# A one-core layer pair whose expert stream is spread over VectorE's steps: four stream pieces a step in tile 2's second attention, and an even tile's projection, norm and queries one step earlier

## The chip, the cores and the metric

The kernel runs on one core of one Trainium2 chip. The metric is the device time of one execution in microseconds (us). Engines: PE is TensorE, DVE is VectorE, ACT is ScalarE, POOL is GpSimd, SP is SyncE.

## What is computed

Two layers in a row over 512 tokens of width 1024, in float32.

```python
x = first_block(x, ...)     # 16 meta tokens, windowed pooling, forgetting attention, gates, norm
h = rms_norm(x, attn_norm); proj = h @ w_in
sb = stick_breaking_attention(sb_q, sb_k, sb_v)         # 8 heads
mla = chunk_causal_softmax_attention(q, k, v)           # 8 heads
x = x + concat(rms_norm(sb), rms_norm(mla)) @ w_o
x = x + peer_ffn(rms_norm(x, ffn_norm), ...)

def peer_ffn(...):                                       # per token
    q = (x @ w_q).reshape(T, 8, 2, 128)
    sc = einsum('thcd,chnd->thcn', q, sub_keys)          # 8 heads, 2 halves, 128 keys
    top_s, top_i = top_k(sc, 16)                         # then the best 16 of 256 pairs
    g = softmax(best_s)
    pre = einsum('td,thkd->thk', x, u[idx])              # 128 rows of u per token
    out = einsum('thk,thkd->td', g * gelu(pre), v[idx])  # 128 rows of v per token
```

u and v have 16384 rows of 1024 numbers each. What bears on the change is the second attention (stick-breaking and softmax), the projection by w_o, the queries of the expert layer, its top-k and its dot products with rows of u.

## The kernel before, in words

**Tiles and groups.** The 512 tokens are four tiles of 128, numbered 0 to 3. Group 0 is tiles 0 and 1, group 1 is tiles 2 and 3. "The third tile" is tile 2. For each group the program runs first_dense, first_attention, first_output, second_dense and second_attention; PE, ACT and DVE each have their own function of that name, with the same loops, and meet at semaphores. After both groups the expert stage proper follows: PE builds weights ("builds") and multiplies streamed tiles of v by them.

**The second attention** has one step for each tile and head, p = 0 to 15 in a group. In a step DVE takes the positive part (L1670), runs the reversed scan (L1672), subtracts (L1678), takes the next head's maximum (L1657, L1658), lets the stream go on by two pieces (`side(2)`), normalises the softmax (L1685, L1686), on an even head copies out the outputs of the two heads before (`outputs`, L1626), and lets the stream go on again. PE forms the scores of head p+2, which wait for DVE's L1678 of head p, then transposes head p's probabilities (L2054), which wait for L1686; it multiplies by the values one step later. ACT has the exponentials and copies the transposed probabilities.

**What rides along in the odd tile's steps.** While tile 1 (or 3) is in its attention, the even tile before it gets its output projection (`project` on PE, four of 8 matmuls of 512 columns, each followed by `combine` on DVE, L1644; all four use one PSUM bank, so a project waits for the combine before it), its norm (`expert_norm` on ACT, `prep_norm` on DVE, L1651), and ten pieces of preparation (`prepare` on PE, `evac_prep` on ACT, L894): two transposes xT, four queries q of 32 matmuls each, four scores s. Three tables say at which head h each stands: PROJECT_AT, PREP_AT and the `h ==` lines. Below, P1, P2 and P3 are the three steps in which PE does three preparations each. The odd tile has the same work after its last head.

**The stream.** `experts()` is a Python generator that emits DVE's expert work piece by piece, and `side(n)` emits the next n pieces at that place in DVE's order. A piece is a dot (L1206, one gathered row of u for each of 128 tokens against the token) or one of the eleven parts of a pair: the top-k of two heads (`prep_pair`, L1122 to L1195). I count these parts 0 to 10. A pair can't begin before its scores are copied out by ACT, and `routed` says from which step it may stand in the order; until then a `side` emits nothing. POOL gathers the rows of u (L656) when a pair has given the indices (L1195). The first 256 dots use six buffers, so a gather waits for the dot six before it.

**The hand-over.** After dot 256 (head-chunk 15) the stream takes a pair (heads 16 and 17), and then, in the program before, nothing until both groups' attention is over. What follows emits 14 dots of chunk 16, the pair of heads 18 and 19, the last two dots of chunk 16, and the first build. The last two rows of chunk 16 go into buffers that are free only when PE's last preparation is done.

Of the kernel before, what the change touches and what calls it, by code (L numbers as in the profile page):

```python
# [24 lines left out]
H = 8  # L25
# [39 lines left out]
def build(nc, a, out):  # L65

    ctx = ExitStack()
    with ctx:
# [146 lines left out]
        KEYS = range(len(gathered), len(gathered) + 2 * (first_at - keys_at) // D)  # L215
# [149 lines left out]
        PREP = [("xT", 0), ("xT", 1), ("q", 0), ("q", 1), ("s", 0), ("q", 2), ("s", 1), ("q", 3), ("s", 2), ("s", 3)]  # L365
        NP = len(PREP)

        PROJECT_AT = {2: (0, 1), 3: (2, 3)}
        PREP_AT = {5: (0, 1, 2), 6: (3, 4, 5), 7: (6, 7, 8)}


        w_in = a["w_in"][0]
# [290 lines left out]
        def _(act):  # L663
# [246 lines left out]
            def second_attention(g):  # L910
# [30 lines left out]
                for p in range(first, end):  # L941
                    i, h = ATT[p]
                    w = (i + 1) * P
                    if p + 1 < end:
                        softplus(p + 1)
                    if p > first:
                        copy_pT2(p - 1, 0)
                        copy_pT2(p - 1, 1)
                    if i % TG:
                        if h == 2:  # L950
                            out_root(i - 1)
                        if h == 4:
                            expert_norm(i - 1)
                        for n in PREP_AT.get(h, ()):
                            evac_prep(i - 1, n)
                    act.wait_ge(ml_max, p + 1)
                    if p:
                        act.wait_ge(pT2_done[1], p)
                    nc.scalar.activation(Pb2[:, 1, 0:w], psum[:, 2 + p % 2, 0:w], ACT.Exp,
                                         bias=stat[:, 96 + p % 4:97 + p % 4], scale=QK ** -0.5,  # L960
                                         accum_out=stat[:, 100 + p % 4:101 + p % 4]).then_inc(exp2_done[1], 1)
                    act.wait_ge(zr_done, p + 1)
                    nc.scalar.activation(Pb2[:, 0, 0:w], Pb2[:, 0, 0:w], ACT.Exp).then_inc(exp2_done[0], 1)
                    if p % 2 == 0 and p > first:
                        squares(p // 2 - 1)
# [3 lines left out]
                i = TG * g + TG - 1  # L969
# [116 lines left out]
        def _(dve):  # L1086
# [23 lines left out]
            routed = [0] * NT  # L1110
# [144 lines left out]
            def experts():  # L1255
                def tops_of(*ks):
                    for k in ks[::2]:
                        while k % H + 1 >= routed[k // H]:
                            yield
                        yield from prep_pair(k // 2)  # L1260
# [7 lines left out]
                    yield from dots(k)  # L1268
                split()
                early_over[0] = True  # L1270
                yield from tops_of(2 * H, 2 * H + 1)
                while not dense_over[0]:
                    yield
                first_rows = dots(16)
                for _ in range(len(KEYS) + 4):
                    next(first_rows)
                yield from tops_of(18, 19)
                for _ in first_rows:
                    pass
                beside = chain(*[dots(k) for k in U_FIRST])  # L1280
                for b in range(BUILDS):
# [73 lines left out]
            def side(n):  # L1355
                for _ in range(n):
                    next(stream, None)
# [260 lines left out]
            def second_attention(g):  # L1618
# [43 lines left out]
                for p in range(first, end):  # L1662
                    i, h = ATT[p]
# [26 lines left out]
                    if i % TG:  # L1690
                        for n in PROJECT_AT.get(h, ()):
                            combine(i - 1, n)
                        if h == 4:
                            prep_norm(i - 1)
                        routed[i - 1] = {5: 2, 6: 6, 7: 8}.get(h, 0)
                        side(6 if h > 4 else 3)
                    else:
                        side(4)
                outputs(end // 2 - 1)
                i = TG * g + TG - 1  # L1700
                mean_squares(i)
# [563 lines left out]
```

## Time and profile before

| What | Value |
|---|---|
| three runs | 2197.37, 2205.95, 2209.19 us; median 2205.95 |
| profiled execution | 2211.92 us, of which the span of its instructions is 2209.9 us |
| PE busy | 1940.1 us (88%) |
| DVE busy | 1383.5 us (63%) |
| POOL busy | 934.9 us (42%) |
| ACT busy | 547.1 us (25%) |
| the chain that ended last | PE 58%, DVE 12%, POOL 11%, issue 7%, DMA 7%, ACT 3% |

Times within the profile are counted from the span's start. The second attention of group 0 stands at about 371 to 508 us (tile 1 from 397), that of group 1 at about 1028 to 1237 us (tile 3 from 1110), and the first build begins at 1309 us. Busy shares are means over stages that differ, so the change has to be read stage by stage. A row of a timeline gives a start, a length, the engine, the line and the operation, and in brackets how long the engine had been idle and who released it.

### The profile page before, as it was taken

What the parts mean: (1) busy time and instruction counts of PE and PEld (TensorE: products, weight loads), DVE (VectorE), ACT (ScalarE), POOL (GpSimd) and SP (SyncE); (2) the same over time, 40 slices, a digit from 0 to 9 for tenths busy, and PEclk for the clock granted to TensorE, in tenths of its full rate; (3) what the DMA queues carried; (4) which work ended last, traced back from release to release, by engine and by line L of the source; (5) the groups of instructions that cost most, each with busy time, mean ns of one, the idle gap of its engine ahead of it and who ended that gap; (6) DMA issues with size and microseconds to landing.
All of it is one profiled execution on the core that took longest, in us unless ns stands there. A gap on an engine that the chain in (4) does not pass through costs nothing.

```text
span 2209.9 us, 22139 instructions
## 1 busy us (share of the span) xinstructions
PE 1940.1 (88%) x7602; PEld 1231.5 (56%) x7602; DVE 1383.5 (63%) x3090; ACT 547.1 (25%) x1520; POOL 934.9 (42%) x814
## 2 busy tenths in 40 slices
PE   6999999887998998967778878899999999997776
PEld 5677666575865665544657666644457644442222
DVE  1111224455878874768986388899779966634554
ACT  2112024322111110212333237600138610011111
POOL 2000000010335562575761246533868864447775
PEclk9999998798998888986588889999999999999999
DMA  5322344155977797798875677899999999989998
GB/s 173 130 97 82 128 158 152 58 189 198 333 271 256 253 342 260 278 383 292 299 269 215 247 276 239 260 340 354 396 409 317 321 409 409 409 347 409 401 410 358
DMA packets 190623, 614.85 MB, mean 278 GB/s; under 512 B 18096, under 2 KB 18096, under 8 KB 190512
## 3 DMA queue, kind: packets, MB, share of 16 engines
q0 software_dynamic: 111168, 403.64, 49.6%
q1 hardware_dynamic: 76400, 202.92, 24.8%
q10 hardware_dynamic: 2944, 6.89, 0.9%
q8 instruction: 61, 1.00, 0.2%
q14 instruction: 50, 0.41, 0.1%
HBM read 610.22 MB, written 3.15 MB: 278 GB/s over the span
## 4 chain that ended last, share of the span: by engine, by line
PE 58%; DVE 12%; POOL 11%; issue 7%; DMA 7%; ACT 3%; ACTq 0%; POOLq 0%; SPq 0%; DVEq 0%
PE ps L1736 57%; POOL sb_arena L656 9%; DVE sb_arena L1206 4%; DMA sb_arena<-in_peer_u,sb_idx 3%; POOL sb_wring L656 2%; ACT sb_arena L1033 1%; DMA sb_wring<-in_w_out 1%; DMA sb_gains<-in_norm_g 1%; DVE sb_arena L1672 1%; PE ps L2054 1%; DMA sb_wring<-in_w_up_attn 1%; DMA sb_wring<-in_w_in 1%; DVE sb_arena L1346 0%; DMA sb_arena<-in_peer_v,sb_idx 0%; DVE sb_arena L1678 0%
## 5 line engine op out<-in xcount | busy, mean ns | idle before, releaser
L656 POOL DMA_INDIRECT sb_arena<-in_peer_u,sb_idx x470 | 602.8, 1283 | 1035.3 <-DVE sb_idx L1195 482.9
L1736 PE MATMUL ps<-sb_wring,sb_arena 128*128 128x512 f32 (+2 forms) x1632 | 699.5, 589 | 41.8 <-DVE sb_arena L1574 18.2
L1206 DVE CUSTOM_DVE_ANT_0 sb_arena<-sb_arena 128x1024 f32<-128x1024 f32 x470 | 562.4, 1222 | 102.0 <-DMA sb_arena<-in_peer_u,sb_idx 98.2
L1736 PEld LDWEIGHTS ps<-sb_wring,sb_arena 128*128 128x128 f32 x1632 | 312.6, 193 | 418.2 <-issue 365.5
L1736 PE MATMUL ps<-sb_arena,sb_wring 128*128 128x256 f32 (+2 forms) x2688 | 512.9, 353 | 14.6 <-ACT sb_arena L894 5.9
L1736 PEld LDWEIGHTS ps<-sb_arena,sb_wring 128*128 128x128 f32 x2688 | 447.8, 199 | 68.7 <-issue 6.5
L1736 PE MATMUL ps<-sb_arena 128*128 128x64 f32 (+9 forms) x1968 | 350.6, 330 | 57.9 <-DVE sb_arena L1678 16.8
L1736 PEld LDWEIGHTS ps<-sb_arena 128*128 128x128 f32 (+4 forms) x1968 | 279.6, 199 | 123.5 <-issue 73.8
L656 POOL DMA_INDIRECT sb_arena<-in_peer_v,sb_idx x192 | 202.8, 1056 | 121.3 <-PE ps L1736 50.3
L1736 PE MATMUL ps<-sb_arena,sb_poolw 128*128 128x512 f32 (+1 forms) x424 | 204.1, 608 | 56.6 <-DMA sb_arena<-in_peer_v,sb_idx 36.2
L1235 DVE SCALAR_TENSOR_TENSOR sb_arena<-sb_arena,sb_coef 128x1024 f32<-128x1024 f32 x90 | 115.5, 1284 | 118.3 <-DMA sb_arena<-in_peer_v,sb_idx 118.0
L1736 PEld LDWEIGHTS ps<-sb_arena,sb_poolw 128*128 128x128 f32 x424 | 74.0, 192 | 161.6 <-ACT sb_poolw L1024 85.0
L1033 ACT ACTIVATE sb_arena<-sb_arena 128x64 f32<-128x64 f32 x512 | 129.2, 335 | 47.8 <-DVE sb_arena L1346 43.2
L1024 ACT ACTIVATE sb_poolw<-sb_ident,sb_coef 128x128 f32<-128x128 f32 x136 | 53.9, 399 | 282.8 <-PE ps L1736 282.8
L1736 PE MATMUL ps<-sb_wring,sb_poolw 128*128 128x512 f32 x136 | 66.3, 610 | 19.2 <-DMA sb_wring<-in_peer_v,sb_idx 14.0
L656 POOL DMA_INDIRECT sb_wring<-in_peer_u,sb_idx x42 | 50.9, 1211 | 75.0 <-PE ps L1736 43.0
L1349 DVE TENSOR_TENSOR sb_arena<-sb_arena,sb_iota 128x1024 f32<-128x1024 f32 x64 | 77.8, 1216 | 0.0
L656 POOL DMA_INDIRECT sb_wring<-in_peer_v,sb_idx x64 | 66.0, 1031 | 26.9 <-issue 14.3
L1001 ACT ACTIVATE sb_coef<-sb_coef 128x16 f32<-128x16 f32 (+1 forms) x18 | 4.0, 225 | 270.7 <-DVE sb_coef L1206 270.6
L1470 DVE TENSOR_REDUCE sb_stat<-ps 128x1 f32<-128x144 f32 (+3 forms) x32 | 16.2, 507 | 79.7 <-PE ps L1736 78.7
L1206 DVE CUSTOM_DVE_ANT_0 sb_wring<-sb_wring,sb_arena 128x1024 f32<-128x1024 f32 x42 | 51.2, 1224 | 15.8 <-DMA sb_wring<-in_peer_u,sb_idx 15.5
L1235 DVE SCALAR_TENSOR_TENSOR sb_arena<-sb_wring,sb_coef,sb_arena 128x1024 f32<-128x1024 f32 x30 | 38.5, 1284 | 34.9 <-DMA sb_wring<-in_peer_v,sb_idx 34.8
(240 smaller groups left out, 1341.3 us busy)
## 6 DMA issues: line engine op xcount, KB each, us to landing
sb_wring<-in_peer_v SPq DMA_DIRECT2D x128, 512.0 KB, 6.8
sb_wring<-in_w_in SPq DMA_DIRECT2D x52, 1024.0 KB, 7.5
sb_wring<-in_peer_w_q SPq DMA_DIRECT2D x32, 1024.0 KB, 7.4
sb_wring<-in_w_o SPq DMA_DIRECT2D x16, 1024.0 KB, 7.1
sb_wring<-in_w_out SPq DMA_DIRECT2D x8, 1024.0 KB, 9.3
sb_arena<-in_peer_u,sb_idx POOLq DMA_INDIRECT x470, 6.6
sb_arena<-in_x ACTq DMA_DIRECT2D x8, 512.0 KB, 7.0
sb_wring<-in_w_up_pool SPq DMA_DIRECT2D x4, 1024.0 KB, 7.2
```

The lines of the kernel that those rows point to most:

```text
L656: nc.gpsimd.indirect_dma_start(gathered[buf(n)], None, table, bass.IndirectOffsetOnAxis(ap=idx[:, t, at_:at_ + 1], axis=0))\
L1001: nc.scalar.activation(coef[:, t, cols], coef[:, t, cols], ACT.Gelu).then_inc(gelu_done, k1 - k0)
L1024: nc.scalar.activation(diag[:, n % 4, :], ident[:], ACT.Copy, scale=coef[:, t, s:s + 1])\
L1033: last = nc.scalar.activation(pick_a[:, b % 2, n, :], pick_a[:, b % 2, n, :], ACT.Copy, scale=rank_t[:, 2 * TG + t, at_ + n:at_ + n + 1])
L1206: nc.vector.tensor_tensor_reduce(out=gathered[buf(n)], in0=gathered[buf(n)], in1=xn[:, t % TG, :], scale=1.0, scalar=0.0, op0=ALU.mult, op ...
L1235: nc.vector.scalar_tensor_tensor(rows_of_tile(t), gathered[buf(n)], coef[:, t, s:s + 1], rows_of_tile(t), ALU.mult, ALU.add).then_inc(vect ...
L1349: nc.vector.tensor_tensor(pick_j[b % 2], second_.to_broadcast([P, PICK, NK]), iota[:].unsqueeze(1).to_broadcast([P, PICK, NK]), ALU.is_equal)\
L1470: nc.vector.tensor_reduce(stat[:, 96 + n % 4:97 + n % 4], s_ps[:, 0:w], AX, ALU.max, negate=True)\
L1672: link(nc.vector.tensor_tensor_scan(suffix[:, w - 1::-1] if w == T else suffix[:, 0:w][:, ::-1], suffix[:, w - 1::-1] if w == T else suffi ...
L1736: return nc.tensor.matmul(o, l, r, start=start, stop=stop)
L2054: last = nc.tensor.transpose(psum[:, 4 + kind, j * P:(j + 1) * P], Pb2[:, kind, j * P:(j + 1) * P], ident[:])
```

## The change

Three things are edited. In the even tile's steps the second `side` gives two pieces in place of four, so a step has four pieces, not six. Tile 0 shares the line, but no score has been formed then and the stream is empty. In the odd tile's steps all four projections stand at head 2 (before: two at head 2, two at head 3), the norm at head 3 (before 4), the preparations at heads 4, 5 and 6 (before 5, 6 and 7), and `side` gives six pieces from head 4 on (before from 5). The pair of heads 18 and 19 stands right behind that of 16 and 17, where the stream may take it during the attention, and the detour before the first build is gone.

```diff
-        PROJECT_AT = {2: (0, 1), 3: (2, 3)}
-        PREP_AT = {5: (0, 1, 2), 6: (3, 4, 5), 7: (6, 7, 8)}
+        PROJECT_AT = {2: (0, 1, 2, 3)}
+        PREP_AT = {4: (0, 1, 2), 5: (3, 4, 5), 6: (6, 7, 8)}
...
-                        if h == 4:
+                        if h == 3:
                             expert_norm(i - 1)
...
-                yield from tops_of(2 * H, 2 * H + 1)
+                yield from tops_of(*range(2 * H, 2 * H + 4))
                 while not dense_over[0]:
                     yield
-                first_rows = dots(16)
-                for _ in range(len(KEYS) + 4):
-                    next(first_rows)
-                yield from tops_of(18, 19)
-                for _ in first_rows:
+                for _ in dots(16):
                     pass
...
-                        if h == 4:
+                        if h == 3:
                             prep_norm(i - 1)
-                        routed[i - 1] = {5: 2, 6: 6, 7: 8}.get(h, 0)
-                        side(6 if h > 4 else 3)
+                        routed[i - 1] = {4: 2, 5: 6, 6: 8, 7: 8}.get(h, 0)
+                        side(6 if h > 3 else 3)
                     else:
-                        side(4)
+                        side(2)
```

Behind the edit the lines of the rest are four lower (L1736 is L1732, L1686 is L1682, L1626 is L1622, L1644 is L1640).

**On PE, group 0, tile 1, from head 2 on.** The rows of 8 matmuls with `sb_wring` and 512 columns are two projections. Before:

```order
L1736 MATMUL ps<-sb_arena 64x128 x4
L1736 MATMUL ps<-sb_wring,sb_arena 128x512 x8
L1736 MATMUL ps<-sb_arena 128x256
L1736 MATMUL ps<-sb_masks,sb_identb 128x128
L1736 MATMUL ps<-sb_arena 128x256
L1736 MATMUL ps<-sb_masks,sb_identb 128x128
L2054 MATMUL ps<-sb_ident,sb_arena 128x128 x4
L1736 MATMUL ps<-sb_ones,sb_arena 128x1 x2
L1736 MATMUL ps<-sb_arena 64x128 x4
L1736 MATMUL ps<-sb_wring,sb_arena 128x512 x8
```

With the change:

```order
L1732 MATMUL ps<-sb_arena 64x128 x4
L1732 MATMUL ps<-sb_wring,sb_arena 128x512 x16
L1732 MATMUL ps<-sb_arena 128x256
L1732 MATMUL ps<-sb_masks,sb_identb 128x128
L1732 MATMUL ps<-sb_arena 128x256
L1732 MATMUL ps<-sb_masks,sb_identb 128x128
L2050 MATMUL ps<-sb_ident,sb_arena 128x128 x4
L1732 MATMUL ps<-sb_ones,sb_arena 128x1 x2
L1732 MATMUL ps<-sb_arena 64x128 x4
```

The four projections now stand together, and head 3's step has none.

**On DVE, group 1, the end of tile 3's attention.** L1685 and L1686 (L1681 and L1682) normalise head 7, L1626 (L1622) is the last `outputs`, L1632 (L1628) the sum of squares that follows. Before:

```order
L1670 TENSOR_SCALAR sb_arena<-ps 128x512
L1672 SCALAR_TENSOR_TENSOR sb_arena<-sb_arena 128x512
L1678 TENSOR_TENSOR sb_arena<-ps,sb_arena 128x512
L1685 RECIPROCAL sb_stat<-sb_stat 128x1
L1686 TENSOR_SCALAR sb_arena<-sb_arena,sb_stat 128x512
L1626 TENSOR_SCALAR sb_arena<-ps,sb_gains 128x128 x2
L1632 TENSOR_REDUCE sb_stat<-ps 128x2
```

With the change, the rows just ahead of the last `outputs`:

```order
L1193 SCALAR_TENSOR_TENSOR sb_arena<-sb_arena 128x2x16
L1195 CAST sb_idx<-sb_arena 128x32
L1122 MAX sb_arena<-sb_arena 128x8 x4
L1126 MAX_INDEX sb_arena<-sb_arena 128x8 x4
L1130 MATCH_REPLACE sb_arena<-sb_arena 128x128 x2
L1138 MAX sb_arena<-sb_arena 128x8 x2
L1142 MAX_INDEX sb_arena<-sb_arena 128x8 x2
L1130 MATCH_REPLACE sb_arena<-sb_arena 128x128 x2
L1138 MAX sb_arena<-sb_arena 128x8 x2
L1622 TENSOR_SCALAR sb_arena<-ps,sb_gains 128x128 x2
L1628 TENSOR_REDUCE sb_stat<-ps 128x2
```

Between head 7's normalise and the last outputs stand six stream pieces now; they are parts 9 and 10 of one pair and 0 to 3 of the next, and two more pieces stand ahead of the normalise.

**On DVE, between the last two combines of tile 3** (L1640), with the change; before, the four combines follow each other:

```order
L1640 SCALAR_TENSOR_TENSOR sb_arena<-ps,sb_stat,sb_arena 128x512
L1176 CAST sb_angle<-sb_arena 128x64
L1177 CAST sb_angle<-sb_arena 128x64
L1179 TENSOR_SCALAR sb_arena<-sb_angle 128x2x16
L1180 SCALAR_TENSOR_TENSOR sb_arena<-sb_angle 128x2x16
L1181 SCALAR_TENSOR_TENSOR sb_arena<-sb_arena,sb_angle 128x2x16
L1184 TENSOR_TENSOR sb_arena<-sb_arena,sb_iota 128x512
L1189 TENSOR_TENSOR sb_arena<-sb_arena,sb_angle 128x512
L1192 TENSOR_REDUCE sb_arena<-sb_arena 128x32
L1184 TENSOR_TENSOR sb_arena<-sb_arena,sb_iota 128x512
L1189 TENSOR_TENSOR sb_arena<-sb_arena,sb_angle 128x512
L1640 SCALAR_TENSOR_TENSOR sb_arena<-ps,sb_stat,sb_arena 128x512
```

These are parts 8 and 9 of the pair of heads 18 and 19. Between the other combines stand parts 4 to 7.

## Rows read from the trace of the kernel before

**Rows 1.** Windows, seven steps of tile 2 (length, PE, PEld, DVE, ACT, POOL, PEclk, DMA, GB/s):
```profile
1037.84:1110.54 72.70, 56.07 (x208) 44.27 (x208) 71.72 (x139) 26.03 (x59) 54.50 (x43) 0.52 0.89 303
```

**Rows 2.** Timeline of DVE, two dots there (start, length, engine, line, operation):
```profile
1070.95 1.22 DVE L1206 CUSTOM_DVE_ANT_0 sb_arena<-sb_arena 128x1024 f32<-128x1024 f32 x1
1072.09 1.22 DVE L1206 CUSTOM_DVE_ANT_0 sb_arena<-sb_arena 128x1024 f32<-128x1024 f32 x1
```

**Rows 3.** Timeline of PE in one step of it: scores and values:
```profile
1070.44 1.64 PE L1736 MATMUL ps<-sb_arena 64*128 64x256 f32 x4 [1.88 <-DVE sb_arena L1678]
...
1076.11 2.79 PE L1736 MATMUL ps<-sb_arena 128*64 128x128 f32 x12
```

**Rows 4.** Timeline of DVE, tile 3, heads 2 to 4: second combine, two scans:
```profile
1141.94 0.75 DVE L1644 SCALAR_TENSOR_TENSOR sb_arena<-ps,sb_stat,sb_arena 128x512 f32<-128x512 f32 x1 [3.79 <-PE ps L1736]
...
1146.76 1.22 DVE L1672 TENSOR_TENSOR_SCAN sb_arena<-sb_arena 128x512 f32<-128x512 f32 x1
...
1161.66 1.22 DVE L1672 TENSOR_TENSOR_SCAN sb_arena<-sb_arena 128x512 f32<-128x512 f32 x1
```

**Rows 5.** Timelines of DVE and PE, tile 3, heads 5 to 7: waits:
```profile
1199.29 0.87 DVE L1122 MAX8 sb_arena<-sb_arena 128x8 f32<-128x128 f32 x4 [10.66 <-ACT sb_arena L894]
...
1210.64 1.97 PE L2054 MATMUL ps<-sb_ident,sb_arena 128*128 128x128 f32 x8 [3.92 <-DVE sb_arena L1686]
...
1230.18 1.43 PE L2054 MATMUL ps<-sb_ident,sb_arena 128*128 128x128 f32 x8 [2.08 <-DVE sb_arena L1686]
```

**Rows 6.** Timeline of DVE, end of tile 3's attention and last combine:
```profile
1229.64 0.49 DVE L1686 TENSOR_SCALAR sb_arena<-sb_arena,sb_stat 128x512 f32<-128x512 f32 x1
...
1236.42 0.61 DVE L1626 TENSOR_SCALAR sb_arena<-ps,sb_gains 128x128 f32<-128x128 f32 x2 [6.29 <-ACT sb_arena L937]
...
1252.60 0.75 DVE L1644 SCALAR_TENSOR_TENSOR sb_arena<-ps,sb_stat,sb_arena 128x512 f32<-128x512 f32 x1 [2.68 <-PE ps L1736]
```

**Rows 7.** Timeline of DVE, the one whole top-k pair before the first build:
```profile
1285.96 0.87 DVE L1122 MAX8 sb_arena<-sb_arena 128x8 f32<-128x128 f32 x4
...
1290.38 0.49 DVE L1138 MAX8 sb_arena<-sb_arena 128x8 f32<-128x128 f32 x2
...
1292.10 0.50 DVE L1154 MAX8 sb_arena<-sb_arena 128x8 f32<-128x136 f32 x2
...
1295.52 0.20 DVE L1176 CAST sb_angle<-sb_arena 128x64 f32<-128x64 uint16 x1
...
1301.27 0.28 DVE L1195 CAST sb_idx<-sb_arena 128x32 uint32<-128x32 f32 x1
```

**Rows 8.** Timelines of DVE and PE, tile 1: scans, last normalise, outputs, sums:
```profile
425.89 0.69 DVE L1672 TENSOR_TENSOR_SCAN sb_arena<-sb_arena 128x256 f32<-128x256 f32 x1
...
437.64 0.69 DVE L1672 TENSOR_TENSOR_SCAN sb_arena<-sb_arena 128x256 f32<-128x256 f32 x1
...
497.76 0.35 DVE L1686 TENSOR_SCALAR sb_arena<-sb_arena,sb_stat 128x256 f32<-128x256 f32 x1
...
507.03 0.60 DVE L1626 TENSOR_SCALAR sb_arena<-ps,sb_gains 128x128 f32<-128x128 f32 x2
...
507.78 0.98 PE L1736 MATMUL ps<-sb_ones,sb_arena 128*128 128x1 f32 x4 [6.31 <-DVE sb_arena L1626]
```

**Rows 9.** Timelines of DVE and POOL at the start of group 1:
```profile
569.82 1.50 DVE L1376 TENSOR_TENSOR sb_arena<-ps,sb_gains 128x512 f32<-128x512 f32 x2 [1.78 <-PE ps L1757]
...
493.67 0.94 POOL L656 DMA_INDIRECT sb_arena<-in_peer_u,sb_idx  x1 [0.30 <-issue]
...
574.70 1.99 POOL L656 DMA_INDIRECT sb_arena<-in_peer_u,sb_idx  x1 [0.30 <-issue]
```

**Rows 10.** The chain that ended last, before the first build (start, length, what):
```profile
1253.88 40.99 issue
...
1296.34 8.37 DMA sb_wring<-in_peer_u,sb_idx
...
1308.78 12.47 PE ps L1736 x52
```

## The prediction

> **What bounds the kernel now.** I read the page's busy shares first (PE 88%), then the chain that ended last, then windows and timelines of the stretches that the change touches. Each attention step is read by the wait that ends last in it.
>
> In tile 2's second attention DVE is the bound. Seven steps take 72.70, a step 10.39, and DVE is busy for 71.72 of them, PE for 56.07 at a granted clock of 0.52, so nearly always at 1.2 GHz [rows 1]. PE waits for L1678 at each scores [rows 3].
>
> In tile 3, heads 2 and 3 are a round trip: DVE waits 3.79 for a projection and combines it in 0.75 [rows 4], and the next projection needs that bank. From head 5 on PE's preparations are the bound: DVE once waited 10.66 for scores to be copied out, with nothing of the stream to do [rows 5]. At the end of both tiles the stream is dry: after the last normalise DVE has only outputs, and waits 6.29 for ACT [rows 6].
>
> The first build, at 1308.78, is reached through POOL's gathers: 40.99 of issue, a landing of 8.37, one dot [rows 10]. From there on (901 us to the end of the span) the change touches nothing, so I carry the difference at the first build to the end.
>
> **The terms.** Times are of the profiled execution (2211.92, which is 5.97 above the median of 2205.95); I add the sum to either. About 0.5%, 11 us, is what a measurement can tell from no change.
>
> 1. *Tile 2, two dots a step fewer.* Two dots start 1.14 apart [rows 2], so DVE's step falls by 2.29 to 8.10. PE's loop is then next: from its scores to the end of its values, where the next scores stand, is 1070.44 to 1078.90, 8.46 [rows 3], without its present wait of 1.88 before the scores. The step becomes 8.46: −1.93 × 8 = **−15.4**. Bounds: −18.3 if DVE still sets it, −13 if the two engines' waits for each other leave 0.3 a step.
>
> 2. *Tile 3, all projections at head 2.* Two more round trips, 2 × (3.79 + 0.75) = 9.1 [rows 4], move to head 2; the step from head 3's scan to head 4's took 14.90 [rows 4]. If the moved trips cover it, two steps shrink together by 14.90 − 9.1 = **−5.8**. In tile 1 the same is 11.75 [rows 8] − 9.1 = **−2.6**.
>
> 3. *Tile 3, preparations from head 4.* The stall of 10.66 goes [rows 5], but PE had preparations to do in most of it: what PE itself lost is its 3.92 before head 6's transposes against 2.08 in the next step [rows 5]. I take **−1.8** (0 to −3.9).
>
> 4. *The last step of tile 3.* The stream is no longer dry there. Between head 6's normalise and the last outputs DVE's order now has, by count, the parts of a whole pair and parts 1 to 3 of another. A pair is 1285.96 to 1301.55, 15.6; its parts 1 to 3 are 1285.96 to 1290.87 less the first 0.87, 4.0 [rows 7]. With 0.2 off for what does not wait, 19.4, plus DVE's own work of about 4.6 (outputs 0.6, the scan group 2.7, normalise 0.65, outputs 0.6), is 24. Before, from that normalise's end at 1230.13 to the outputs' end at 1237.03 was 6.9 [rows 6]. So the last outputs come **+17** later. Queued behind the pieces are the last normalise, for which PE's transposes wait, and the last outputs, for which PE's sum of squares waits, with tile 3's projection behind it. Nothing is late enough elsewhere to cover it.
>
> 5. *Between the last combines.* The last gap becomes parts 8 and 9, 1295.52 to about 1300.2, 4.7 [rows 7], against an idle 2.68 before [rows 6]: **+2.0**. The gaps before hold cheaper parts, which fit the round trip.
>
> 6. *The last step of tile 1.* The same with a whole pair (15.4) and parts 5 to 7 (3.4 [rows 7]), and own work of 3.2: 22. Before: 498.11 to 507.63, 9.5 [rows 8]. **+12.5**. PE already waited 6.31 for these outputs [rows 8], so nothing covers it either.
>
> 7. *The seam between the groups.* The stream goes into group 1 eight pieces ahead. What stood there was 22 parts and 2 dots; now it is 14 parts and 10 dots in a row, with six buffers. The seventh dot's gather is issued when the first dot is over: POOL needs 1.99 and 0.30 a gather beside dots, 0.94 when DVE is in none [rows 9], and a landing takes 8.37 [rows 10]. Six dots of 1.14 last 6.9, so the seventh waits 3 to 6; DVE has 1.78 of slack before it [rows 9]. **+3** (0 to +6).
>
> 8. *The pair of heads 18 and 19 before the first build.* DVE is rid of 15.6 of work at 1285.96 [rows 7], but the chain there goes over POOL's issue and the landing, not over DVE's pairs [rows 10]: **0**. If the chain could start earlier, at most DVE's part of it, some −4. The gathers into the last two buffers still wait for PE's last preparation, which follows tile 3's projection.
>
> Group 1: −15.4 − 5.8 − 1.8 + 17 + 2 = −4.0. Group 0 and seam: −2.6 + 12.5 + 3 = +12.9. Sum **+9**, so 2205.95 + 9 = **2215** by the median, 2221 by the profiled execution. The change pays in tile 2 and pays back in the two last steps, where it puts VectorE's stream in front of work that PE waits for.
>
> SBUF: by the Trainium skill (SBUF — State Buffer, "Who interferes with whom") a VectorE instruction with two SBUF inputs contends with a GpSimd instruction that reads SBUF, and the later one stands until the first is done. The gathers' 1.99 against 0.94 agree with it [rows 9]; by that rule ten dots in a row are the dearest place for gathers, and with the undisturbed 0.94 the seam would cost about 1 in place of 3.
>
> **The rivals.**
>
> *A, the last steps are covered.* ACT's copies of the last preparations and PE's own step could be what the last outputs wait for, as in tile 3 before (6.29 for ACT [rows 6]); then DVE's pieces fill idle time. Terms 4 to 6 would fall away: 9 − 31.5 = −22.5, 2183. Against it: DVE's count of 24 and 22 is of work alone, and the idle it can fill is 6.29 and already counted. If only half is covered it gives about 2199. Chance 0.15.
>
> *B, slower: gathers can't keep up with dots in a row.* Place: the ten dots at the seam. If every one of the last eight waits for POOL's cadence of 2.29 instead of 1.14 [rows 2, 9], that is 9.2 and not 3, sum +15, 2221; with term 1 at −13 it is +18, 2224. It decides against me from a seam cost of 5 on, as the sum is then past 11. For: POOL is busy 54.50 of 72.70 even at six pieces [rows 1]. Against: the first six rows are there before. Chance 0.20.
>
> *C, PE's clock rises in tile 2.* PE was granted 0.52 with 56.07 of 72.70 busy [rows 1]. With steps of 8.46, PE would hardly idle, and if it is granted 2.4 GHz its loop falls well under 8.10 and DVE stays the bound: −18.3, sum +6, 2212. Against: PE's work was interrupted at every scores [rows 3] and would be still. Chance 0.10. The Trainium skill (TensorE: Matmul & The Clock Gate, "A second HAM failure mode: psum-queue depth-cycling") says that frequent short idle times between groups of matmuls can keep the clock swinging between its two levels; the 0.52 of the row agrees, and by that rule tile 2 stays at the low level as long as PE waits in every step.
>
> *That the change does not do what it says* is excluded for the projections, the pieces and the pairs by the rows of the order; only tile 0, whose stream is empty, doesn't feel the smaller number.
>
> **How the numbers follow.** The forecast case has 0.55. With terms 1, 3, 4 and 7 at their ends it reaches from 2207 to 2224, and it lies at 0.34 within 0.5%, at 0.20 slower and at 0.01 faster. Rival A gives 0.15 faster, B 0.20 slower, C 0.08 within and 0.02 slower. That makes faster 0.16, same 0.42, slower 0.42. The range is 2198 to 2229: below, half of rival A; above, B with another 5 for the medians' scatter (the three runs lie 11.8 apart).
>
> **What would show it.** In the changed kernel's profile: scans of tile 2 about 8.5 apart (10.39 before); no wait of 10.66 for scores in tile 3; the last outputs of group 0 ending near 517 (507.63), with PE waiting some 12 to 17 for them; those of group 1 near 1246; waits of DVE for gathers among the dots right behind group 0; the first build near 1318 (1308.78) and 901 us from there to the end. I am wrong if the outputs at the end of tile 1 come no later than 510 (rival A), if the seam costs over 5 (B), if tile 2 has a granted clock well above 0.52 (C), or if the first build moves by something other than the outputs before it, which would mean that term 8 is not 0.

## The result and the profile after

The changed kernel took 2225.09 us (median of 9 runs, 2208.93 to 2228.67), the kernel before 2206.93 (9 runs, 2197.37 to 2213.66). The ratio is 1.0078, with a 95% interval of 1.0055 to 1.0101: 17 us slower. On a second chip it was 1.0069 (1.0044 to 1.0093). I had forecast 9 us slower; the way it went was right, and its size is twice the forecast's.

The two profiled executions (2211.92 and 2225.09) are read by landmarks. A step is counted from one head's scan to the next.

| Landmark | before | after | late by | of it new |
|---|---|---|---|---|
| last combine of tile 1 | 525.3 | 542.0 | 16.7 | +16.7 |
| first scan of tile 2's second attention | 1027.2 | 1051.0 | 23.8 | +7.1 |
| first scan of tile 3's | 1110.5 | 1115.8 | 5.3 | −18.5 |
| last combine of tile 3 | 1252.6 | 1268.7 | 16.1 | +10.8 |
| first build | 1308.8 | 1325.7 | 16.9 | +0.9 |
| PE's last instruction | 2205.0 | 2218.3 | 13.3 | −3.6 |

**Tile 2.** The windows of its seven steps (columns as in [rows 1]):

```profile
1059.35:1115.83 56.48, 46.29 (x211) 37.61 (x210) 55.51 (x111) 25.90 (x60) 35.39 (x28) 0.69 0.77 253
```

A step takes 8.07 in place of 10.39 [rows 1]. DVE is busy for 55.51 of 56.48, so it still is the bound, and PE was granted 0.69 and not 0.52.

**The steps of heads 2 and 3.** Timeline of DVE, the scans of heads 2, 3 and 4 in tile 1; head 2's of before; and the same four in tile 3 (the others of before are in [rows 4] and [rows 8]):

```profile
407.27 0.69 DVE L1668 TENSOR_TENSOR_SCAN sb_arena<-sb_arena 128x256 f32<-128x256 f32 x1
...
434.80 0.69 DVE L1668 TENSOR_TENSOR_SCAN sb_arena<-sb_arena 128x256 f32<-128x256 f32 x1
...
441.45 0.69 DVE L1668 TENSOR_TENSOR_SCAN sb_arena<-sb_arena 128x256 f32<-128x256 f32 x1
```

```profile
407.60 0.69 DVE L1672 TENSOR_TENSOR_SCAN sb_arena<-sb_arena 128x256 f32<-128x256 f32 x1
```

```profile
1135.80 1.22 DVE L1668 TENSOR_TENSOR_SCAN sb_arena<-sb_arena 128x512 f32<-128x512 f32 x1
...
1163.44 1.22 DVE L1668 TENSOR_TENSOR_SCAN sb_arena<-sb_arena 128x512 f32<-128x512 f32 x1
...
1174.91 1.22 DVE L1668 TENSOR_TENSOR_SCAN sb_arena<-sb_arena 128x512 f32<-128x512 f32 x1
```

```profile
1130.51 1.22 DVE L1672 TENSOR_TENSOR_SCAN sb_arena<-sb_arena 128x512 f32<-128x512 f32 x1
```

Head 2's step grew from 18.3 to 27.5 in tile 1 and from 16.2 to 27.6 in tile 3. Head 3's step shrank, but only from 11.8 to 6.6 and from 14.9 to 11.5. So the two together are longer with the projections packed. With them each odd tile can be split by its scans:

| Stretch | tile 1 before | tile 1 after | tile 3 before | tile 3 after |
|---|---|---|---|---|
| first scan to head 2's | 9.7 | 9.7 | 20.0 | 20.0 |
| head 2's to head 4's | 30.0 | 34.2 | 31.2 | 39.1 |
| head 4's to the last combine | 87.7 | 100.6 | 90.9 | 93.8 |

**The end of tile 1.** Timeline of DVE, from head 6's normalise to the last outputs, and of PE, which waits twice there:

```profile
502.03 0.35 DVE L1682 TENSOR_SCALAR sb_arena<-sb_arena,sb_stat 128x256 f32<-128x256 f32 x1
...
515.55 0.35 DVE L1682 TENSOR_SCALAR sb_arena<-sb_arena,sb_stat 128x256 f32<-128x256 f32 x1
...
523.42 0.61 DVE L1622 TENSOR_SCALAR sb_arena<-ps,sb_gains 128x128 f32<-128x128 f32 x2
```

```profile
515.96 1.12 PE L2050 MATMUL ps<-sb_ident,sb_arena 128*128 128x128 f32 x4 [10.43 <-DVE sb_arena L1682]
...
524.17 0.97 PE L1732 MATMUL ps<-sb_ones,sb_arena 128*128 128x1 f32 x4 [2.96 <-DVE sb_arena L1622]
```

From 502.38 to 524.03 are 21.7. The 9.5 of [rows 8] is not the same place: it starts at head 7's normalise. Head 6's of before is this row:

```profile
480.38 0.35 DVE L1686 TENSOR_SCALAR sb_arena<-sb_arena,sb_stat 128x256 f32<-128x256 f32 x1
```

From its end, 480.73, to 507.63 are 26.9, with PE's last three preparations in them. So this stretch became 5.2 shorter, not longer; from head 7's normalise on it is 8.1 in place of 9.5. What the pieces do cost shows in PE: it has no preparation left for this step and stands for 10.43 and 2.96, where it stood 1.80 and 6.31 before.

**The first preparation step of tile 1.** Timeline of PE, transposes and first query:

```profile
445.05 1.12 PE L2114 MATMUL ps<-sb_ident,sb_arena 128*128 128x128 f32 x4 [0.68 <-ACT sb_arena L894]
446.89 10.06 PE L1732 MATMUL ps<-sb_arena,sb_wring 128*128 128x128 f32 x64 [0.72 <-ACT sb_arena L894]
```

The 64 matmuls took 10.06; in the profile of the kernel before, taken again in experiment 11, they took 7.38 and the transposes 0.65 instead of 1.12. Over the 32 us from the first transpose the granted clock was 0.86 here and 1.00 there.

**The seam.** Timeline of DVE, two of the ten dots behind group 0:

```profile
579.10 1.22 DVE L1206 CUSTOM_DVE_ANT_0 sb_arena<-sb_arena 128x1024 f32<-128x1024 f32 x1
...
582.97 1.23 DVE L1206 CUSTOM_DVE_ANT_0 sb_arena<-sb_arena 128x1024 f32<-128x1024 f32 x1 [2.64 <-DMA sb_arena<-in_peer_u,sb_idx]
```

Six dots run without a wait, and the seventh waits 2.64.

**The end of tile 3.** Timeline of DVE, the last two normalises, the last outputs and the last combine; then PE:

```profile
1228.20 0.49 DVE L1682 TENSOR_SCALAR sb_arena<-sb_arena,sb_stat 128x512 f32<-128x512 f32 x1
...
1242.99 0.49 DVE L1682 TENSOR_SCALAR sb_arena<-sb_arena,sb_stat 128x512 f32<-128x512 f32 x1
...
1251.61 0.61 DVE L1622 TENSOR_SCALAR sb_arena<-ps,sb_gains 128x128 f32<-128x128 f32 x2
...
1268.67 0.75 DVE L1640 SCALAR_TENSOR_TENSOR sb_arena<-ps,sb_stat,sb_arena 128x512 f32<-128x512 f32 x1
```

```profile
1243.53 1.97 PE L2050 MATMUL ps<-sb_ident,sb_arena 128*128 128x128 f32 x8 [9.43 <-DVE sb_arena L1682]
```

From 1228.69 to 1252.22 are 23.5. Here too the 6.9 of [rows 6] starts at head 7's normalise, and head 6's of before is this row:

```profile
1210.09 0.49 DVE L1686 TENSOR_SCALAR sb_arena<-sb_arena,sb_stat 128x512 f32<-128x512 f32 x1
```

From its end to 1237.03 are 26.5, so this stretch is 3.0 shorter, and from head 7's normalise on it is 8.7 in place of 6.9. PE stands for 9.43 in front of head 7's transposes, 2.08 before [rows 5]. The last combine starts 5.2 after the one at 1263.46 and waits for nothing but the pieces in front of it; before it followed after 3.4 with an idle 2.68 [rows 6].

### The profile page after: what moved, and what is told of

Read it like the earlier page. It is cut to its first block, busy times and chain, and to the rows that moved or that the text cites. A ratio compares the mean times of both kernels' runs of the same rounds, so it can differ in the third digit from the quotient of the medians.

```text
span 2223.3 us, 22142 instructions
## 1 busy us (share of the span) xinstructions
PE 1938.9 (87%) x7602; PEld 1231.5 (55%) x7602; DVE 1382.9 (62%) x3090; ACT 547.3 (25%) x1520; POOL 935.7 (42%) x814
## 3 DMA queue, kind: packets, MB, share of 16 engines
q0 software_dynamic: 111168, 403.64, 49.0%
## 4 chain that ended last, share of the span: by engine, by line
PE 59%; DVE 12%; POOL 10%; DMA 8%; issue 7%; ACT 4%; ACTq 0%; POOLq 0%; DVEq 0%; SPq 0%
PE ps L1732 57%; POOL sb_arena L656 8%; DMA sb_arena<-in_peer_u,sb_idx 3%; DVE sb_arena L1206 3%; POOL sb_wring L656 2%; ACT sb_arena L1033 1%; DMA sb_arena<-in_peer_v,sb_idx 1%; DMA sb_wring<-in_w_out 1%; DMA sb_gains<-in_norm_g 1%; PE ps L2050 1%; DMA sb_wring<-in_w_up_attn 1%; DVE sb_arena L1668 1%; DMA sb_wring<-in_w_in 1%; DVE sb_arena L1342 0%; DVE sb_arena L1184 0%
## 5 line engine op out<-in xcount | busy, mean ns | idle before, releaser
L1732 PE MATMUL ps<-sb_wring,sb_arena 128*128 128x512 f32 (+2 forms) x1632 | 697.1, 588 | 44.6 <-DVE sb_arena L1570 18.7
L1732 PEld LDWEIGHTS ps<-sb_wring,sb_arena 128*128 128x128 f32 x1632 | 311.8, 192 | 420.7 <-issue 365.2
L1732 PE MATMUL ps<-sb_arena,sb_wring 128*128 128x256 f32 (+2 forms) x2688 | 519.5, 356 | 16.6 <-ACT sb_arena L894 5.9
L1732 PEld LDWEIGHTS ps<-sb_arena,sb_wring 128*128 128x128 f32 x2688 | 454.2, 202 | 71.3 <-issue 9.7
L1732 PE MATMUL ps<-sb_arena 128*128 128x64 f32 (+9 forms) x1968 | 344.8, 326 | 50.1 <-ACT sb_arena L1033 13.7
L1732 PEld LDWEIGHTS ps<-sb_arena 128*128 128x128 f32 (+4 forms) x1968 | 275.2, 197 | 113.4 <-issue 75.3
L1732 PE MATMUL ps<-sb_arena,sb_poolw 128*128 128x512 f32 (+1 forms) x424 | 203.6, 606 | 60.2 <-DMA sb_arena<-in_peer_v,sb_idx 35.0
L1732 PEld LDWEIGHTS ps<-sb_arena,sb_poolw 128*128 128x128 f32 x424 | 73.6, 191 | 164.6 <-ACT sb_poolw L1024 86.5
L1732 PE MATMUL ps<-sb_wring,sb_poolw 128*128 128x512 f32 x136 | 66.3, 610 | 19.1 <-DMA sb_wring<-in_peer_v,sb_idx 13.9
L656 POOL DMA_INDIRECT sb_wring<-in_peer_v,sb_idx x64 | 64.1, 1001 | 26.7 <-issue 14.3
L1466 DVE TENSOR_REDUCE sb_stat<-ps 128x1 f32<-128x144 f32 (+3 forms) x32 | 16.2, 506 | 79.7 <-PE ps L1732 79.4
L2050 PE MATMUL ps<-sb_ident,sb_arena 128*128 128x128 f32 x160 | 34.9, 370 | 33.2 <-DVE sb_arena L1682 33.2
```

Of the source, the lines that this page charges most:

```text
L656: nc.gpsimd.indirect_dma_start(gathered[buf(n)], None, table, bass.IndirectOffsetOnAxis(ap=idx[:, t, at_:at_ + 1], axis=0))\
L1466: nc.vector.tensor_reduce(stat[:, 96 + n % 4:97 + n % 4], s_ps[:, 0:w], AX, ALU.max, negate=True)\
L1732: return nc.tensor.matmul(o, l, r, start=start, stop=stop)
L2050: last = nc.tensor.transpose(psum[:, 4 + kind, j * P:(j + 1) * P], Pb2[:, kind, j * P:(j + 1) * P], ident[:])
```

## The experiments

Twelve kernels ran (there is no 6 or 7) in three sets of four, each set on a chip of its own with runs of the kernel before beside it. These chips took 2232 to 2237 for the kernel before, not 2207; the difference lies behind the first build (build to PE's end 914 to 935 there, 896 and 893 in the two profiles above). So totals are compared as ratios, and places by landmarks up to the first build.

**1. Tile 2 alone** (the kernel before, `side(4)` in the else branch to `side(2)`).

> The kernel before, with only the even tile's second side reduced from four pieces to two. Theory (the loss lies in the last steps of tiles 1 and 3 and needs the moved tables; tile 2 alone is a gain): group 0 as before (last outputs at 507.6), tile 2's steps fall from 10.39 to about 8.1 (-18), tile 3 has dots in the places where its stream was dry, next to PE's preparations at heads 5 to 7, and gives back about 3 to 5 there and 2 at the last combine. First build 12 to 14 earlier than 1308.8, median about 2194. Rival (the 16 dots taken from tile 2 come back in full on the path in tile 3, whatever the tables): first build within 3 of before, median about 2207.

Ratio 0.9989 (0.9955 to 1.0023). Tile 2 took 64.85 for its eight steps (83.37 before), so −18.5. Tile 3 gave back 7.6 (149.65 from its first scan to its last combine, 142.06 before, 138.3 in the profile of experiment 11; its first preparations ran at a granted 0.86, not 1.00, so not all of the 7.6 need be the dots'), and a new stall came behind it: 68.6 from the last combine to the first build, where it was 56.2. Timeline of PE in the last preparations, and of POOL, first of 14 gathers in a row (the last at 1255.73):

```profile
1249.48 0.36 PE L1736 MATMUL ps<-sb_arena,sb_wring 128*128 128x128 f32 x1 [0.61 <-issue]
1251.60 0.37 PE L1736 MATMUL ps<-sb_arena,sb_wring 128*128 128x128 f32 x1 [1.76 <-issue]
1253.70 0.37 PE L1736 MATMUL ps<-sb_arena,sb_wring 128*128 128x128 f32 x1 [1.73 <-issue]
1256.49 0.37 PE L1736 MATMUL ps<-sb_arena,sb_wring 128*128 128x128 f32 x1 [2.42 <-issue]
```

```profile
1239.60 0.94 POOL L656 DMA_INDIRECT sb_arena<-in_peer_u,sb_idx  x1 [43.48 <-DVE sb_idx L1195]
```

The 16 dots push the pair of heads 16 and 17 back, and its 14 gathers run beside the last preparations, where PE stands between single matmuls for "issue". My theory had the gain and the direction but not this stall; the rival had the total.

**2. The tables alone** (the odd tile's tables, `h ==` lines and `h > 3`; tile 2 and the pairs as before).

> The kernel before, with only the odd tile's tables changed (four projections at head 2, norm at head 3, preparations at heads 4 to 6, six pieces from head 4 on); tile 2 keeps four pieces and the pair of heads 18 and 19 its old place. Theory: group 0 and the seam lose as in the changed kernel (last outputs of group 0 at about 524, the first step of tile 2's second attention about 22 to 24 late), tile 2 gains nothing, tile 3's stream is dry from head 5 on, so its last step costs little: first build about 18 late, median about 2225. Rival (the loss in group 0 is an accident of PE's granted clock in that profile, and the tables cost nothing there): last outputs of group 0 near 510, median about 2207.

Ratio 1.0116 (1.0069 to 1.0163); last combine of tile 1 at 541.2, tile 2's first scan at 1048.9, tile 3 in 144.95, first build at 1332.8. Group 0 and the seam came as in the changed kernel, as the theory said; the total lost more than its 0.8%, and tile 3 gained nothing though its stream was dry. By its scans tile 3 lost 8.0 in the steps of heads 2 and 3 (39.1 in place of 31.2) and gained 5.0 behind them (85.9 in place of 90.9).

**3. No pieces in the last step.**

```diff
-                        side(6 if h > 3 else 3)
+                        side(0 if h == 7 else 6 if h > 3 else 3)
```

> The changed kernel, with no stream pieces in the second slot of head 7 of an odd tile (two pieces fewer than six, in both groups: none). Theory (pieces in front of the last outputs are on the path): last outputs of group 0 about 4 to 7 earlier than 524.0, those of group 1 about 1.5 earlier relative to head 6, the last combine no longer 2 late, seam 0 to 3 cheaper; first build 8 to 12 earlier than 1325.7, median about 2213. Rival (the pieces only move to a place where they cost the same): 2224 as the changed kernel.

Ratio 1.0010 (0.9976 to 1.0043), 0.7% under the changed kernel. From head 7's scan to tile 1's last combine 23.5 in place of 29.7: the 6.1 are the six pieces, so they lie on the path, as forecast. From there to tile 2's first scan 493.5 (509.0 in the changed kernel). The first build at 1301.9 still has the stall of the first experiment in it (68.6).

**4. The pair of heads 18 and 19 in its old place.**

> The changed kernel, with the pair of heads 18 and 19 back in its old place between the dots of chunk 16. Theory (where that pair stands costs nothing before the first build, as the gathers set it): group 0 and tile 2 as in the changed kernel, last outputs of tile 3 about 1.5 and last combine about 1.8 more early, first build 3 earlier, median about 2221. Rival (the early pair is worth its 15.6 of VectorE time before the first build): first build 10 or more later, median about 2235.

Ratio 1.0049 (1.0015 to 1.0084). Last combine to first build 55.4 (57.1 in the changed kernel): the pair's place costs nothing before the build that one profile could tell, and gains nothing, as I had it.

**5. The 16 dots where VectorE is idle** (first experiment, and in group 1's first_output):

```diff
+                        if g and s == 0 and c == 0:
+                            side(4)
...
-                    side(3)
+                    side(12 if g and c == 3 else 3)
...
+                        if g and t == 0 and e == 0:
+                            side(3)
```

> The kernel before, with tile 2's second side reduced to two pieces, and the 16 dots that this leaves over placed in group 1's first_output, where VectorE waits for TensorE (9.19, 15.66 and 6.08 at 841.5, 882.9 and 889.7 in the trace of before): four after the first up product, nine more after the last merge, three between the first two residual sums. The stream then reaches tile 3 as in the kernel before. Theory (tile 2's gain is real and is lost only because the 16 dots come back in tile 3 and push the pair's gathers into the last preparations): tile 2's eight steps take 64.9, not 83.4, first_output costs 0 to 4, tile 3 as before (142 from its first scan to the last combine), no stall of TensorE for issue after it; ratio about 0.993 (0.991 to 0.995). Rival (dots in a row starve for gathers, whose queue is shared with the weights): 8 or more lost in first_output, ratio 0.996 to 1.0.

Ratio **0.9931** (0.9903 to 0.9959). Tile 2 64.9, tile 3 145.5, and 56.1 to the first build. The gathers now start at 1221.32 and the 128 matmuls of the same place run through:

```profile
1243.63 17.00 PE L1740 MATMUL ps<-sb_arena,sb_wring 128*128 128x128 f32 x128 [0.88 <-ACT sb_arena L894]
```

So tile 2's gain holds once its dots have another place, and the stall goes with the time of the gathers. The rival took the gathers and the weights to be in one queue; the page lists them in two, q0 (software_dynamic), which has the 403.64 MB of all gathers, and q1 (hardware_dynamic).

**8. The projections alone** (four at head 2, the norm at head 3, preparations still at heads 5 to 7).

> The kernel before, with only the four projections at head 2 and the norm at head 3; preparations stay at heads 5 to 7. Theory (two steps with a round trip of projections become one with four; the combines hide nothing): group 0 and group 1 each within 2 of before at the last outputs, ratio 0.999 to 1.001. Rival (packing them is the gain that I costed at -5.8 and -2.6, and the move of the preparations spoils it): first build 6 to 8 earlier, ratio 0.996.

Ratio 1.0071 (1.0042 to 1.0100). Both theories fell. From head 2's scan to head 4's tile 1 took 34.1 and tile 3 36.6 (30.0 and 31.2 before). In the profile the first build came only 4 late (1312.7), and so I repeated it below with the kernel before beside it. Windows of tile 1, from the last projection to the first preparation, and 32 us from there:

```profile
434.12:449.58 15.46, 13.84 (x63) 10.24 (x63) 9.78 (x26) 9.04 (x26) 0.00 (x0) 0.67 0.63 234
449.58:481.58 32.00, 27.73 (x227) 25.52 (x226) 8.29 (x44) 5.99 (x15) 0.00 (x0) 1.00 0.37 132
```

The light stretch is long and at 0.67, but the preparation behind it was granted 1.00.

**9. The changed kernel with the preparations back at heads 5 to 7.**

> The changed kernel, with the preparations and the six pieces back at heads 5 to 7. Theory (the move of the preparations puts a step of pure VectorE work at the end of tiles 1 and 3 and the stream eight pieces ahead): last combine of tile 1 near 525 (before) and not 542, no extra loss up to group 1's second attention, tile 2 at 64.9; in tile 3 the 16 late dots delay the pair of heads 16 and 17 as in the first experiment; ratio to before 0.999, 0.8% under the changed kernel. Rival (the loss of group 0 is TensorE's clock after the packed projections): last combine of tile 1 at 535 or later.

Ratio 1.0056 (1.0028 to 1.0084). Last combine of tile 1 at 529.9, tile 2's first scan 498.7 later, 64.9 in tile 2, 68.0 of the stall: the landmarks were near the theory's (of the 4.6 by which tile 1's last combine is late, 4.1 lie in the steps of heads 2 and 3), but the total was not. It is the first experiment (0.9989) with the projections packed (and the pair early), and 0.7% slower than that.

**10. The changed kernel again.**

> The changed kernel itself, on the same chip as the others, for a second profile of it. Theory: ratio 1.007 to 1.009, last combine of tile 1 at 536 to 542 (the first preparation step 32 or 37 long, by the clock that TensorE is granted in it), tile 2 64.9, first build about 17 later than in before. Rival (the low clock of that step belongs to the changed order): it is 37 again each time.

Ratio 1.0069; last combine of tile 1 at 540.4, tile 2 64.9. The first preparation step of tile 1 took 36.0: neither 32 nor quite 37, and on the rival's side.

**11. The kernel before.**

> The kernel before itself, for a profile of it on the chip of the other three: both theories 0.998 to 1.002. It gives the base for the landmarks: from tile 1's last combine to tile 2's first scan 496 to 502, first preparation step of tile 1 31.4 long at a granted clock of 1.00, and 56 from tile 3's last combine to the first build.

Ratio 0.9999 (0.9968 to 1.0030). First build at 1304.9, 3.9 earlier than in the first profile of it: that is how far one profile can be trusted. 500.0 from tile 1's last combine to tile 2's first scan, 55.5 from the last combine to the build.

**12. The projections alone, again.**

> The kernel before with only the projections packed and the norm earlier, once more, since its profile (first build 4 late) told less than its median (0.7%). Theory (packing them leaves TensorE short of work in the steps of heads 3 and 4, so that it enters the first preparation step at a lower granted clock): ratio 1.004 to 1.008, tile 1's first preparation step near 36 with a clock under 0.9. Rival (noise of one comparison): ratio 0.998 to 1.003 and a step of 31.4.

Ratio 1.0074 (1.0046 to 1.0102), the same loss a second time. The first build came at 1324.6, 19.7 after that of the kernel before on the same chip. Windows of tile 1 (columns as in [rows 1]): first the kernel before, from the end of the last projection to the first preparation, and 32 us from there; then the same two with the projections packed:

```profile
436.66:444.88 8.22, 6.47 (x41) 4.49 (x41) 5.63 (x15) 6.08 (x18) 0.00 (x0) 1.00 1.01 360
444.88:476.88 32.00, 27.72 (x227) 25.51 (x226) 10.08 (x49) 5.99 (x15) 0.00 (x0) 1.00 0.40 153
```

```profile
435.44:450.76 15.32, 13.69 (x63) 10.06 (x63) 9.78 (x26) 9.06 (x26) 0.00 (x0) 0.67 0.67 237
450.76:482.76 32.00, 28.41 (x212) 26.07 (x212) 5.85 (x34) 5.34 (x13) 0.00 (x0) 0.89 0.39 132
```

Two steps of small matmuls (heads 3 and 4) now lie between PE's heavy pieces of work, 15.3 in place of 8.2. The granted clock falls in them (0.67, where it was 1.00), and here the preparation starts at a lower clock and gets through 212 matmuls in 32 us, not 227. The long light stretch at 0.67 is in all three profiles of this order (8, 9 and 12), but the slow preparation only in this one: the other two got through 227 at 1.00. Their first preparation step is longer (35.9) because the preparation starts 4.3 behind its scan and not 0.2 ahead of it, while the step before it is 3.9 shorter. In tile 3 the stretch from the last projection to the first preparation is 28.3 in place of 14.3, at 0.74 and not 1.00 (in the first profile of the kernel before it was 16.4, at 0.79):

```profile
1157.06:1171.31 14.25, 10.60 (x73) 8.51 (x73) 13.97 (x27) 8.91 (x18) 6.71 (x6) 1.00 1.04 397
```

```profile
1157.51:1185.83 28.32, 21.72 (x112) 18.05 (x111) 27.83 (x50) 13.15 (x26) 16.29 (x11) 0.74 0.87 299
```

**13. Pieces in the combines' gaps** (fifth experiment, and in tile 1 the six pieces of head 7 moved behind the last outputs, two before each combine).

> The kernel of the fifth experiment (tile 2 at four pieces, 16 dots in first_output), and in tile 1 the six pieces in front of the last outputs moved behind them, two before each of the four combines; the seam gives eight for ten, so the stream stands the same afterwards. Theory (pieces in front of the last outputs are on the path, pieces in a combine's round trip are mostly hidden): last outputs of tile 1 5 to 6 earlier, last combine 4 to 5 earlier (the part with the wide compares costs 1 in its gap), ratio 0.990 to 0.992. Rival (same work, same cost): 0.993.

Ratio 0.9928 (0.9898 to 0.9958). Head 7's scan to the last outputs 4.2 shorter than in the fifth, to the last combine 3.2 shorter, as forecast; but group 1's stretch up to tile 2 was 505.1 (499.7), and the median shows no gain over the fifth experiment that can be told from none.

**14. The changed kernel with the 16 dots in idle places.**

> The changed kernel, with the same 16 extra dots in first_output as in the fifth experiment, so that tile 3's stream is dry at its end again. Theory: group 0 and the seam as in the changed kernel, tile 2 at 64.9, tile 3 from its first scan to its last combine 145 in place of 153 (as with the tables alone), 56 to the first build; first build 6 to 9 earlier than in the changed kernel, ratio 1.003 to 1.005. Rival (the last step of tile 3 costs nothing): as the changed kernel, 1.007.

Ratio 1.0067 (1.0033 to 1.0101). Tile 3 took 150.4 (152.8), the stretch before tile 2 517.4 (509.0): inconclusive. What was saved in tile 3 is less than foreseen, and the dots weren't free behind a stream that is eight pieces ahead.

## Why the prediction was half right

**Sum and sign.** +9 forecast, +17 measured (ratio 1.0078); 2225 lies in the range of 2198 to 2229. "Same, within 0.5%" and "slower" had 0.42 each; it was the latter. The likeliest case's own range ended at 2224. That the sum came this near is in good part luck: two parts of it, packing the projections and the last steps, were wrong by about 20 us each, in opposite directions.

**Rival A** (the last steps are covered) fell as stated: PE stood 10.43 and 2.96 in tile 1's last step and 9.43 in tile 3's, and the third experiment got 6.1 back for six pieces. But the last steps cost much less than terms 4 and 6 said, as shown below.

**Term 1 (tile 2, −15.4)** measured −18.5: the bound at which DVE still sets the step, that is rival C's result. The step's PE loop was priced at 8.46 from a row at a clock of 0.52 [rows 1, 3]; with a granted 0.69 it fits below DVE's 8.1. By the Trainium skill (TensorE: Matmul & The Clock Gate, "A second HAM failure mode: psum-queue depth-cycling") frequent idle times keep the clock swinging between its levels; the 0.69 agrees, since it is between 0.5 and 1.0, but it is no reason to price a step at the low level only.

**Term 2 (tile 3 −5.8, tile 1 −2.6)** is a step that failed, in its sign. "If the moved trips cover it, two steps shrink together" lets head 3's step vanish under the round trips that went to head 2. They did come to head 2, 9.2 more in tile 1 and 11.4 in tile 3, but head 3's step kept 6.6 and 11.5 of its own. Together that is +4.1 and +8.0. The steps of heads 0 and 1, which have no projections, take 5.7 and 4.0 in tile 1 and 10.2 and 9.8 in tile 3: that is about what a step costs by itself. Before the change two round trips (9.1) stood in head 3's step and it took 11.8 and 14.9, so they had hidden 4.0 and 5.7 of it. In tile 1 these two steps took 28.0 to 30.3 in the five profiles with the projections apart and 32.1 to 34.3 in the nine with them packed; in tile 3 30.9 to 31.2 (35.8 in one) and 36.6 to 39.1. The means differ by 4.2 and 6.0. Alone, twice, packing cost 0.7% (1.0071, 1.0074), which is about 15 us, and once more on top of the first experiment (0.9989 to 1.0056): some 10 of the 15 lie in these steps.

**Terms 4 and 6 (the last steps, +17 and +12.5)** had the right place and a wrong base. They counted DVE's work from head 6's normalise on (24 and 22; measured 23.5 and 21.7), and took off a stretch of before that starts at head 7's normalise (6.9 and 9.5), which the prediction calls head 6's. The stretch from head 6's on was 26.5 and 26.9 before, since PE's last three preparations stood in it, and the change takes them out. From head 4's scan to the last combine, where the pieces, the earlier preparations and the last combines all lie, tile 3 lost 2.8; terms 3 to 5 had +17.2 for it. Tile 1 lost 12.9 there, 6.0 of it in the first preparation step, so 6.9 is left for term 6. That pieces in front of the last outputs lie on the path is shown by the third experiment, and term 5 held (the last gap grew by 1.8). In tile 3 the errors of terms 2 and 4 cancel, +11.4 forecast and +10.8 measured for terms 2 to 5, and that is luck.

**What had no term: the clock of tile 1's first preparation step.** It took 37.3, 36.0, 36.1 and 37.3 in four profiles with the changed tables, at 0.86 over 32 us, and 32.0 in two, at 1.00; before 31.4. All six have the same order of instructions up to there. I can't tie it to the packing: with packed projections and late preparations one of three profiles had a slow start (0.89), and in tile 3 two of five profiles with the projections apart had one (0.86, first and fifth experiment) against one of nine with them packed. What decides it stays open; in the two profiles compared above it is 6.0 of the 17.

**Term 7 (the seam, +3, up to 6)** was undersized. At L1376, the place that I read, it is 2.5 between the two profiles above and 4.5 between those of experiments 1 and 2. But the eight pieces ahead go on costing behind it: the same instructions are about 10 late from 190 to 250 us behind tile 1's last combine, and 7.1 late at tile 2. From tile 1's last combine to tile 2's first scan four profiles with the stream eight ahead took 502.5 to 509.0 (mean 507.0), six with the stream as before 495.4 to 501.9 (mean 498.1): +9. With the stream two ahead (third experiment) it was 493.5. Rival B's price was right in size and wrong in place: a wait of 2.64 for the seventh dot and shorter ones behind it, but most of the 9 comes later. Which waits make it up there I did not follow.

**Term 8** (0) measured +0.9, and the fourth experiment, whose ratio is 0.2% under the changed kernel's and inside its interval, agrees that the pair's place doesn't matter before the build. I had not thought of the other thing that this place holds: when the pair of heads 16 and 17 ends decides when 14 gathers run.

**The parts by ratio**: tile 2 alone 0.9989, projections alone 1.0071 and 1.0074, all tables 1.0116, all of the change 1.0078 and 1.0069. The table edit is the loss; tile 2's edit is a gain of 0.7% if its dots get another place, and none that can be told if they don't.

**Sum by stretches**, forecast and measured: term 2 −8.4 and +12.1; the last steps with term 3 (terms 3 to 6) +29.7 and +9.7; the clock 0 and +6.0; tile 2 −15.4 and −18.5; the seam +3 and +7.1; behind the last combine 0 and +0.9. That is +9 and +17.

## What to carry to other kernels

Work that is taken out of a bound step has to be given a place where its engine waits, and its followers (here a burst of 14 gathers) move with it; without that the gain comes back later under another name. Round trips that are packed into one step uncover the own work of the step that they leave: a step that is rid of its waits doesn't vanish, it falls to what a step without them takes, and the trace of the kernel before has such steps to read it from (here heads 0 and 1). When a stretch is compared with itself before and after, both ends must be the same landmark. Where two parts of an edit are independent, time them apart: here tile 2's part was worth −0.1% by itself and −0.7% with a place for its dots, and the tables' part +1.2%.

## What the hardware showed that I had not expected

- A burst of 14 gathers beside TensorE's last preparations made it stand for "issue" between single matmuls (0.6 to 2.4 us each) and cost 12 us from last combine to build in three of three profiles (68.6, 68.6, 68.0 against 55.4 to 57.1 in the eleven others). There the gathers begin 5.8 to 8.0 behind tile 3's last combine (experiments 1, 9 and 3); in the eleven others they begin 15.0 to 19.9 ahead of it, and PE never stands for "issue" in the last preparations. The page lists queues of the kind "instruction" among the DMA queues, and the DMA engines moved about 400 GB/s there; but in the fifth experiment they moved 391 GB/s beside the first 9.9 us of the same matmuls, which ran through, so that rate alone is not the cause. That fetched instructions came late is my reading, and no run isolated it.
- The same order of instructions got a first preparation step of 32.0 or of 36 to 37 us in different executions, at a granted 1.00 or 0.86.
- The stage behind the first build, which none of the edits touches, took 893 to 935 us in different profiles. A single profile's end says nothing about an edit of 10 us here; landmarks and medians do.
